# Expert weight units handed over in halves between the splitting engines and TensorE

## The reference

```python
logits = (t @ router).astype(jnp.float32)
top_v, top_i = lax.top_k(logits, TOP_K)            # TOP_K = 2 of 8 experts
gates = jax.nn.softmax(top_v, axis=-1)
...
for e in range(N_EXPERTS):
    out = out + comb[:, e:e + 1] * swiglu(t, wg[e], wu[e], wd[e])

def swiglu(h, wg, wu, wd):                          # 1024 -> 1408 -> 1024
    return (jax.nn.silu(h @ wg) * (h @ wu)) @ wd
```

## Time and profile before

| | |
|---|---|
| Median of 3 runs | 1463.5 us |
| The runs | 1463.50, 1463.55, 1457.72 us |
| The profiled execution's own time | 1458.68 us |
| Its span in the profile | 1457.1 us |
| TensorE busy | 1309.0 us (90%), 5901 matmuls |
| VectorE busy | 938.3 us (64%) |
| ScalarE busy | 709.3 us (49%) |
| Mean granted TensorE clock | 0.963 of full speed |
| First matmul of item 0, last of item 7 | 926.48 us, 1422.92 us |

### The profile page before, as it was taken

The page is one execution under the profiler, slowest core; times in us unless marked ns, Lnnn a source line. Parts: engine busy times, 40 slices in busy tenths (PEclk is TensorE's granted clock), DMA queues, the critical chain, the costliest instruction groups (busy, mean ns, idle before and its releaser), DMA issues.

```text
span 1457.1 us, 16745 instructions
## 1 busy us (share of the span) xinstructions
PE 1309.0 (90%) x5901; PEld 1041.5 (71%) x5901; DVE 938.3 (64%) x1315; ACT 709.3 (49%) x1068; POOL 117.8 (8%) x158
## 2 busy tenths in 40 slices
PE   1897989799999999997988997899999999999990
PEld 1775447688888788876774474778887878788880
DVE  5956781665565457457476516686687668667885
ACT  4444441632122132136345514485687568657884
POOL 1370060000000000003300000200000000000002
PEclk9999999999999999998999998899999999999995
DMA  9931332146454464463542000797699679868995
GB/s 337 337 124 32 138 121 72 60 131 212 149 183 164 145 217 154 157 218 85 222 168 82 6 29 0 289 385 268 229 306 351 209 237 365 280 218 287 371 385 187
DMA packets 142632, 288.05 MB, mean 198 GB/s; under 512 B 6974, under 2 KB 48492, under 8 KB 142572
## 3 DMA queue, kind: packets, MB, share of 16 engines
q1 hardware_dynamic: 132172, 252.39, 49.9%
q0 software_dynamic: 10256, 34.87, 6.7%
q10 hardware_dynamic: 144, 0.00, 0.0%
HBM read 266.01 MB, written 21.23 MB: 197 GB/s over the span
## 4 chain that ended last, share of the span: by engine, by line
PE 78%; DVE 10%; ACT 5%; issue 4%; DMA 2%; ACTq 0%; POOL 0%; SPq 0%; DVEq 0%; POOLq 0%
PE ps L602 19%; PE ps L604 19%; PE ps L603 19%; PE ps L614 3%; PE ps L956 3%; PE ps L955 3%; DVE acc L1452 3%; PE ps L764 2%; PE ps L783 2%; PE ps L743 2%; ACT spl L1293 1%; PE ps L752 1%; DVE spl L1849 1%; DMA x<-in_x 1%; DMA mraw<-in_moe_w_down 1%
## 5 line engine op out<-in xcount | busy, mean ns | idle before, releaser
L1849 DVE TENSOR_TENSOR spl<-mraw,spl 128x1024 fp32r<-128x1024 f32 (+2 forms) x288 | 311.5, 1130 | 86.4 <-ACT spl L1293 85.5
L1293 ACT ACTIVATE spl<-mraw 128x1024 fp32r<-128x1024 f32 (+2 forms) x288 | 266.3, 979 | 118.1 <-PE ps L956 91.4
L1093 ACT ACTIVATE spl<-raw 128x2048 fp32r<-128x2048 f32 (+2 forms) x56 | 100.7, 1799 | 233.1 <-PE ps L604 194.9
L602 PE MATMUL ps<-hT,spl 128*128 128x512 f32 x416 | 164.7, 396 | 8.1 <-DVE hT L1513 8.1
L1436 DVE TENSOR_TENSOR spl<-raw,spl 128x2048 fp32r<-128x2048 f32 (+2 forms) x56 | 120.7, 2158 | 74.7 <-ACT spl L1093 74.1
L603 PE MATMUL ps<-hT,spl 128*128 128x512 f32 x416 | 163.4, 393 | 0.0
L604 PE MATMUL ps<-hT,spl 128*128 128x512 f32 x416 | 163.4, 393 | 0.0
L602 PE MATMUL ps<-spl,xgT 128*128 128x512 f32 (+1 forms) x384 | 147.1, 383 | 14.7 <-DVE spl L1849 11.8
L604 PE MATMUL ps<-spl,xgT 128*128 128x512 f32 (+1 forms) x384 | 144.4, 376 | 0.0
L603 PE MATMUL ps<-spl,xgT 128*128 128x512 f32 (+1 forms) x384 | 144.3, 376 | 0.0
L1452 DVE SCALAR_TENSOR_TENSOR acc<-raw,cond,acc 128x512 f32<-128x512 f32 x154 | 118.7, 771 | 5.4
(11 more groups left out here) (323 smaller groups left out, 2311.4 us busy)
## 6 DMA issues: line engine op xcount, KB each, us to landing
raw<-in_w_mod SPq DMA_DIRECT2D x48, 1024.0 KB, 6.0
mraw<-in_moe_w_down SPq DMA_DIRECT2D x40, 1024.0 KB, 7.8
mraw<-in_moe_w_gate SPq DMA_DIRECT2D x34, 1024.0 KB, 6.6
mraw<-in_moe_w_up SPq DMA_DIRECT2D x34, 1024.0 KB, 6.7
mraw<-in_moe_w_gate SPq DMA_DIRECT2D x16, 768.0 KB, 6.5
mraw<-in_moe_w_up SPq DMA_DIRECT2D x16, 768.0 KB, 7.8
raw<-in_ffn_w_gate SPq DMA_DIRECT2D x11, 1024.0 KB, 8.2
raw<-in_ffn_w_up SPq DMA_DIRECT2D x11, 1024.0 KB, 5.2
```

The lines of the kernel that those rows point to most:

```text
L602: mm(o, lh, rh, start=start, stop=False)
L1093: A(spl[:, s % SPLS, 0, 0:n], raw[:, r % RAWS, 0:n], ACT.Copy).then_inc(hi_ready, 1)
L1293: A(spl[:, (SB + j) % SPLS, 0, c], mraw[:, j % MRAWS, c], ACT.Copy).then_inc(half_ready, 1)
L1849: ins = V.tensor_tensor(o[:, 1, c], mraw[:, j % MRAWS, c], o[:, 0, c].bitcast(F32), ALU.subtract)
```

## The change

Both hand-overs become one count for each half of a unit. In the expert stage `lo_ready` and `w_used` now rise by 2 for each unit, 36 in an item, and all waits for them are renumbered.

- VectorE adds one to `lo_ready` after each of the two low halves, in `part` and in the mixer's two units.
- TensorE's loop over a unit gets an inner loop over its halves q: it waits for the half's low part, does that half's matmuls of tile 0 and then of tile 1, and adds one to `w_used`. In a two-tile item the order is therefore 6, 4, 6, 4 matmuls and not 12, 8. The waits that stood at a tile's first matmul in a unit stand at its first one in the first half.
- ScalarE waits for `w_used` ahead of each high half, for the same half of the unit three before. For unit 2 of an item it waits for the whole of the last unit ahead of both halves.
- A half's columns in `spl` start at 0 and at D = 1024 whatever the unit's size, so that halves of units of different size share their place. Sizes, transfers and the number of matmuls, copies and subtractions stay.

```diff
 # SyncE
-                    eng.wait_ge(lo_ready, i * EU + (SB + j - MRAWS + 1))
+                    eng.wait_ge(lo_ready, i * (2 * EU) + (SB + 2 * (j - MRAWS + 1)))
 # GpSimd
-                eng.wait_ge(lo_ready, i * EU + (SB + EU + 2))
+                eng.wait_ge(lo_ready, i * (2 * EU) + (SB + 2 * EU + 4))
 # TensorE, item
-                def unit(j, k, w):
-                    eng.wait_ge(lo_ready, i * EU + (SB + j + 1))
-                    return unit_of(SB + j, k, w)
+                def half_unit(j, q, k, n):
+
+                    eng.wait_ge(lo_ready, i * (2 * EU) + (SB + 2 * j + q + 1))
+                    v = spl[:, (SB + j) % SPLS, :, D * q:D * q + k * n].rearrange("p h (k n) -> p h k n", k=k)
+                    return lambda kk: (v[:, 0, kk], v[:, 1, kk])
...
-                            u = unit(4 * c + 2 * part + kh, 4, w)
-                            for b in range(tiles):
-                                if c + part + kh == 0:
-                                    eng.wait_ge(xg_ready[b], count[b] + 1)
-                                if c and kh == 0:
-                                    eng.wait_ge(e_mul[b] if part else (e_silu[0], gate_sum)[b], count[b] * 3 + c)
-                                for kk in range(4):
-                                    k = 4 * kh + kk
-                                    last = product(b, ps[:, 2 * b + part, 0:w], xgT, xhT, k, u(kk, 0, w),
-                                                   k == 0, k == KD - 1)
-                            last.then_inc(w_used, 1)
+                            j = 4 * c + 2 * part + kh
+                            for q in range(2):
+                                u = half_unit(j, q, 2, w)
+                                for b in range(tiles):
+                                    if c + part + kh + q == 0:
+                                        eng.wait_ge(xg_ready[b], count[b] + 1)
+                                    if c and kh + q == 0:
+                                        eng.wait_ge(e_mul[b] if part else (e_silu[0], gate_sum)[b], count[b] * 3 + c)
+                                    for kk in (2 * q, 2 * q + 1):
+                                        k = 4 * kh + kk
+                                        last = product(b, ps[:, 2 * b + part, 0:w], xgT, xhT, k, u(kk % 2),
+                                                       k == 0, k == KD - 1)
+                                last.then_inc(w_used, 1)
...
-                    u = unit(j, step, D)
-                    for b in range(tiles):
-
-                        eng.wait_ge(aT_ready[b], count[b] * 3 + (3 if f0 >= 8 else 2))
-                        for q in range(step):
-                            for h in range(2):
-                                last = product(b, ps[:, 4 + 2 * b + h, :], aT, ahT, f0 + q, u(q, 512 * h, 512),
-                                               f0 + q == 0, f0 + q == NB - 1)
-                    last.then_inc(w_used, 1)
+                    parts = [(q, h) for q in range(step) for h in range(2)]
+                    for q in range(2):
+                        u = half_unit(j, q, step, 512)
+                        for b in range(tiles):
+                            if q == 0:
+                                eng.wait_ge(aT_ready[b], count[b] * 3 + (3 if f0 >= 8 else 2))
+                            for at_, (f, h) in enumerate(parts[step * q:step * q + step]):
+                                last = product(b, ps[:, 4 + 2 * b + h, :], aT, ahT, f0 + f, u(at_),
+                                               f0 + f == 0, f0 + f == NB - 1)
+                        last.then_inc(w_used, 1)
 # ScalarE, part
-                    eng.wait_ge(w_used, i * EU + (SB + j - SPLS + 1))
                     w = unit_size(j % EU)
                     for q in range(2):
+                        eng.wait_ge(w_used, i * (2 * EU) + (SB + 2 * (j - SPLS) + (2 if j == 2 else q + 1)))
                         c = slice(w // 2 * q, w // 2 * q + w // 2)
-                        A(spl[:, (SB + j) % SPLS, 0, c], mraw[:, j % MRAWS, c], ACT.Copy).then_inc(half_ready, 1)
+                        A(spl[:, (SB + j) % SPLS, 0, D * q:D * q + w // 2], mraw[:, j % MRAWS, c], ACT.Copy).then_inc(half_ready, 1)
 # VectorE, part
-                        ins = V.tensor_tensor(o[:, 1, c], mraw[:, j % MRAWS, c], o[:, 0, c].bitcast(F32), ALU.subtract)
-                    ins.then_inc(lo_ready, 1)
+                        to = slice(D * q, D * q + w // 2)
+                        V.tensor_tensor(o[:, 1, to], mraw[:, j % MRAWS, c], o[:, 0, to].bitcast(F32),
+                                        ALU.subtract).then_inc(lo_ready, 1)
```

More of the change, by code:

```diff
@@ L1309, in silu @@
                     def silu(c):
-                        eng.wait_ge(w_used, i * EU + (SB + 4 * c + 2))
+                        eng.wait_ge(w_used, i * (2 * EU) + (SB + 8 * c + 4))
                         w = EW[c][1]
@@ L1326, in up_half @@
                     def up_half(c):
-                        eng.wait_ge(w_used, i * EU + (SB + 4 * c + 4))
+                        eng.wait_ge(w_used, i * (2 * EU) + (SB + 8 * c + 8))
                         w = EW[c][1]
@@ L1359, in item @@
                             rows(1, next_pair + 1)
-                    eng.wait_ge(w_used, i * EU + (SB + EU))
+                    eng.wait_ge(w_used, i * (2 * EU) + (SB + 2 * EU))
                     eng.wait_ge(ye_free, i + 1)
@@ L1696, in mixer @@
                             eng.wait_ge(half_ready, 2 * j + q + 1)
-                            ins = V.tensor_tensor(o[:, 1, c], mraw[:, j, c], o[:, 0, c].bitcast(F32), ALU.subtract)
-                        ins.then_inc(lo_ready, 1)
+                            V.tensor_tensor(o[:, 1, c], mraw[:, j, c], o[:, 0, c].bitcast(F32), ALU.subtract).then_inc(
+                                lo_ready, 1)
             def dense():
```

## The result

The changed kernel takes 1446.4 us in the median of 4 runs (1445.0 to 1448.7), the kernel before 1462.6. The ratio of the fast runs is 0.9902, 95% interval 0.9881 to 0.9923: 14.3 us faster, between 11.3 and 17.4 (the two medians lie 16.2 us apart). The forecast was a median of 1452.1 in a range of 1444.5 to 1460.5, and 11.4 us of gain. The profiled execution took 1445.0 us itself (span 1443.4), 13.7 less than the profiled one of before, and that difference can be followed item by item.

A forecast was written before the change was run, and what follows sets the result against it. TensorE held 78% of the chain, with 11.8 us of waits for low parts to attack. Terms of 8.2 us plus 3.2 from the clock took 1458.7 to 1447.3; keeping 4.8 gave 1452.1 us, range 1444.5 to 1460.5.

The forecast's parts named there:

- Forward by halves: TensorE starts after the first of two low halves; 1.13 us off each wait at least that long.
- Backward by halves: ScalarE fills a slot's first half while TensorE reads the second; 0.37 us earlier at items 3 and 5, 0.14 in item 0.
- there nothing can be gained inside: Inside two-tile items, TensorE busy for 79.37 of 79.39 us, so no gain there.
- Item 0: Item 1's start 1.13 + 0.14 = 1.27 us earlier; unit 2's gain lost to the wait for `aT` at unit 12.
- as long as before: Item 0 up to its last matmul keeps its length, with the wait for `aT` at unit 12 grown.
- Items 6 and 7: The whole short wait for VectorE's low part goes in each: 0.50 and 0.64 us, together 1.14.
- The clock: Shorter waits ahead of items 3 and 5 bring no clock fall in unit 0: 2 x 1.61 = 3.2 us gained.
- What is added: 144 more increments and 144 more waits on TensorE, more on VectorE and ScalarE too, cost 0 each.
- a restart: Rival, chance 0.05: mid-unit semaphores break the matmul stream; 0.10 us 144 times, 14.4 us, a net loss of 3.0.
- a small price: Rival, chance 0.05: each added mid-unit increment and wait costs 0.03 us, 4.3 us in all, giving 1456.4.
- The end: After the last matmul ScalarE copies `ye` sooner, its unneeded split being done first: about 0.54 us gained.
- The median: Forecast 1452.1 us: the profiled 1447.3 with the old 4.8 us between profiled execution and median kept.

The follow-up runs named there:

- Forward only: The changed kernel, but ScalarE waits for both halves of the slot ahead of the first high half; ratio to the kernel before 0.9946.
- the filled wait: The kernel before with nine useless matmuls (2.0 us) in TensorE's wait ahead of each two-tile item; ratio to the kernel before 0.9987.

## Why the prediction was right

**Forward by halves**, 1.13 us a wait: right. The waits at unit 2 of items 2 and 4 fell by 1.14 (1.50 to 0.36). Items 2 and 4 gained 2.76 and 2.68 where 2.63 had been worked out, and that TensorE would not run into the second halves held: no new wait appeared in them.

**Backward by halves**, 0.37 us a wait: right in kind, short in size. It is 0.49, and in two-tile items 0.22 us hung on it that the forecast denied ("there nothing can be gained inside"). That sentence is the step that failed. It rested on 79.37 busy of 79.39 us, and busy time hardly shows a wait of the length of a matmul's modelled tail, 0.39 - 0.23 = 0.16 us. The trace of before had the wait, in the row of weight loads shown above. Why the wait between items fell by 0.49 and not by 0.37 is not shown. All in all the backward part is worth 2.6 us with the end, where its terms were 0.14, 2 x 0.37 and 0.54, together 1.4.

**Item 0** gained 1.35 (forecast 1.27), in part by luck, for two misses offset each other. The wait ahead of item 1 fell by 1.05 (2.23 to 1.18) and not by 1.27. And unit 2's gain was lost at unit 12 only in the main, 1.34 us less wait there and 1.04 more here: 0.30 were kept, where 0 was forecast. From the first matmul to the last, item 0 takes 51.85 us and not 52.14, though it was to be "as long as before".

**Items 6 and 7** gained 1.07 and 0.14: the two waits somewhat less than the 1.14 worked out for them, and inside item 7 a little that no row of waits had listed. Forward only has it too (item 7 in 47.06 us).

**The clock**: 3.25 us against 3.2, and the filled wait shows its cause. The one choice that could have gone the other way, no fall after the shorter waits, held for waits of 1.18, 0.57 and even 1.7 us.

**What is added** costs nothing, right, shown with some three times as much of it on TensorE (144 and 272 more); what ScalarE and VectorE got was not tested by itself. The rivals of a restart and of a small price are out.

**The end**: 0.48 against 0.54.

**The median.** 1452.1 was 5.7 too high. The sum in the profile was 1.0 short inside the expert layer (12.4 for 11.4), and I put it on a median 4.8 us above the profiled execution, which the changed kernel's isn't (1446.4 and 1445.0). As far as the runs show, clock falls outside the items, and where item 0 starts, set how far a run lies above its best; keeping the distance was a choice without a row behind it. The ratio's interval, 11.3 to 17.4 us, includes the sum at its lower edge.

## What to carry to other kernels

When two engines hand a buffer over whole, a consumer's wait at a boundary contains the producer's second half, and splitting the count removes that much (1.14 us of 1.50 here). The working asks that half a unit of the consumer outlasts half a unit of the producer (here 1.38 against 1.13 us); no run had it the other way round. Count what hangs on a wait of TensorE beside its length: here 3.2 of the 12.4 us gained in the layer were the slower clock behind two waits of 2.2 us. Matmuls that compute nothing of use, put into the wait, bring that part back alone. Take the starts of matmuls and the waits of the weight loads, not the busy share, to say that TensorE never waits.

## What the runs showed that was not expected

In the chain of the changed kernel's second profile, ahead of item 0:

```profile
920.61 1.37 DVE xfull L1932 x4
921.98 7.27 another core or an unknown queue
...
929.28 1.38 DVE xfull L1932 x4
```

In that profile and in the changed kernel's first one, TensorE's gathering of these rows:

```profile
913.91 10.16 PE L1036 MATMUL ps<-pick,xn 128*128 128x128 f32 x64 [1.41 <-DVE pick L1795]
```
```profile
912.28 10.15 PE L1036 MATMUL ps<-pick,xn 128*128 128x128 f32 x64 [1.40 <-DVE pick L1795]
```

VectorE stands for 7.3 us between two halves of the first rows. By the program its second half (L1930) waits for the 64th of these matmuls (L1039), which ends at 913.91 + 10.16 = 924.07. VectorE starts at 929.28, so 5.2 us of the 7.3 are explained by nothing in the program. In the first profile the 64th ends at 922.43 and VectorE starts at 922.48: the stop of 2.1 us there is the wait for TensorE, though the profile names no releaser. The 5.2 us are the whole difference between the waits of 8.02 and 2.85 us ahead of item 0. Profiles taken together agree, whatever the kernel: four and two have the long stop, three the short one, as do the first two profiles, before and after. So it doesn't come from the change. The same chip number stands beside long and short stops, so it isn't fixed to the chip either. What VectorE waits for in the 5.2 us is open. The start of item 0 comes that much later, but the transfers run on meanwhile, and item 0 is then 2.2 us shorter (51.25 us for 53.42).
